# Expert stage of a two-layer decoder step: the next expert's rows are turned behind gate and up

## The reference

```
hid = silu(einsum('td,edf->tef', hf, w_gate)) * einsum('td,edf->tef', hf, w_up)
y   = einsum('tef,efd->td', hid * gate[..., None], w_down)
```

## Time and profile before

| what | value |
|---|---|
| median of 3 runs | 1547.96 us |
| the profiled execution | 1544.7 us |
| its span, first to last instruction | 1542.9 us |
| mean granted TensorE clock | 0.905 of full speed |
| TensorE busy with matmuls | 1246.5 us (81%) |
| VectorE, ScalarE, GpSimd busy | 567.9, 412.2, 168.8 us |
| GU in all 32 steps | 240.6 us busy, 44.5 us idle before it |
| moved by DMA | 270.85 MB, 176 GB/s over the span |

### The profile page before, as it was taken

The page is one execution under the profiler, slowest core; times in us unless marked ns, Lnnn a source line. Parts: engine busy times, 40 slices in busy tenths (PEclk is TensorE's granted clock), DMA queues, the critical chain, the costliest instruction groups (busy, mean ns, idle before and its releaser), DMA issues. The chain is left out here.

```text
span 1542.9 us, 22257 instructions
## 1 busy us (share of the span) xinstructions
PE 1246.5 (81%) x8931; PEld 1090.5 (71%) x8931; DVE 567.9 (37%) x1008; ACT 412.2 (27%) x861; POOL 168.8 (11%) x129
## 2 busy tenths in 40 slices
PE   1799999987999855888871999948997963888890
PEld 1799999986999755777751999924336953777770
DVE  2321223339522240111124537688665342111115
ACT  4423244442312320000013522237444240000002
POOL 0300000005000001000002017750000002000002
PEclk9899999998999957999995899958998956999995
DMA  8572322221232105888884138770551205888855
GB/s 242 218 265 82 108 84 83 82 95 50 68 106 83 55 28 212 325 323 326 326 295 156 56 126 285 246 255 28 197 185 64 75 0 221 298 321 318 320 214 203
DMA packets 113405, 270.85 MB, mean 176 GB/s; under 512 B 11094, under 2 KB 69742, under 8 KB 105134
## 3 DMA queue, kind: packets, MB, share of 16 engines
q1 hardware_dynamic: 92768, 230.77, 42.1%
q0 software_dynamic: 9424, 33.13, 5.7%
q10 hardware_dynamic: 11142, 5.96, 1.4%
HBM read 225.43 MB, written 44.40 MB: 175 GB/s over the span
## 5 line engine op out<-in xcount | busy, mean ns | idle before, releaser
L998 PE MATMUL ps<-hT_parts,wh 128*128 128x260 f32 x1152 | 326.8, 284 | 0.0
L1144 PE MATMUL ps<-U,ring 128*128 128x128 f32 x2048 | 240.6, 279 | 44.5 <-DVE U L1604 44.5
L1144 PEld LDWEIGHTS ps<-U,ring 128*128 128x128 f32 x2048 | 234.8, 194 | 52.1 <-issue 33.5
L1366 DVE TENSOR_TENSOR ring_parts<-ring,wh 128x1024 fp32r<-128x1024 f32 x104 | 136.6, 1315 | 263.0 <-ACT wh L710 263.0
L996 PE MATMUL ps<-x_parts,wh 128*128 128x260 f32 x768 | 219.6, 286 | 8.7 <-ACTq L749 7.9
L998 PEld LDWEIGHTS ps<-hT_parts,wh 128*128 128x128 f32 x1152 | 218.5, 190 | 0.0
L997 PE MATMUL ps<-x_parts,ring_parts 128*128 128x260 f32 x768 | 217.3, 283 | 0.0
L996 PE MATMUL ps<-V_parts,wh 128*128 128x260 f32 x512 | 147.8, 289 | 8.2 <-DVE U_parts L1482 5.2
L996 PEld LDWEIGHTS ps<-x_parts,wh 128*128 128x128 f32 x768 | 145.3, 189 | 9.1 <-ACTq L749 8.0
L997 PE MATMUL ps<-V_parts,ring_parts 128*128 128x260 f32 x512 | 146.5, 286 | 0.0
L997 PEld LDWEIGHTS ps<-x_parts,ring_parts 128*128 128x128 f32 x768 | 145.2, 189 | 0.0
(11 more groups left out here) (250 smaller groups left out, 1757.1 us busy)
## 6 DMA issues: line engine op xcount, KB each, us to landing
ring<-in_w_e_gate SPq DMA_DIRECT2D x32, 1024.0 KB, 5.0
ring<-in_w_e_up SPq DMA_DIRECT2D x32, 1024.0 KB, 7.7
ring<-in_w_e_down SPq DMA_DIRECT2D x32, 1024.0 KB, 8.6
ring<-in_w_uv SPq DMA_DIRECT2D x24, 1024.0 KB, 5.6
U<-slots_dram SPq DMA_DIRECT2D x32, 512.0 KB, 5.7
slots_dram<-U SPq DMA_DIRECT2D x32, 512.0 KB, 8.9
ring<-in_cache_k SPq DMA_DIRECT2D x32, 512.0 KB, 4.4
ring<-in_cache_v SPq DMA_DIRECT2D x32, 512.0 KB, 5.2
```

Source lines behind the costliest of these rows:

```text
L998: ins = pe.matmul(to, wh[:, chunk % 2, c, :], rhs_l(c, half), start=False, stop=last and c == DC - 1)
L1144: ins = pe.matmul(ps[:, 2 + q, f * SLOTS:(f + 1) * SLOTS], w[:, c, (f % 2) * P:(f % 2 + 1) * P], xsT[:, q, c, :], start=c == 0, stop=c == ...
L1366: e.tensor_tensor(low_parts(b, half), w, plain(wh[:, chunk % 2]), ALU.subtract).then_inc(split_lo, 1)
```

## The change

In three lists two neighbours change places, in the loop and in the experts written out ahead of it. On TensorE T(e+1) goes ahead of D(e-1), on VectorE evac(e+1) goes ahead of `y_half`(e-1), and on SyncE rows(e) goes ahead of the load of gate(e). No instruction is added or taken away, and the waits in front of each are the same; ScalarE's and GpSimd's lists do not change.

```diff
@@ SyncE, experts @@
                     else:
+                        load_rows(0, 2)
                         load(b, wg[2], (DC, DE))
-                        load_rows(0, 2)
                         load(b + 1, wu[2], (DC, DE))
                         load(b + 2, wd[1], (2, D))
                 with sp.Fori(0, 6) as i:
                     for k in range(2):
                         b = base + 8 + 3 * k
+                        load_rows(i, 3 + k)
                         load(b, one(wg, i * 2 + (3 + k)), (DC, DE), i, 2)
-                        load_rows(i, 3 + k)
                         load(b + 1, one(wu, i * 2 + (3 + k)), (DC, DE), i, 2)
                         load(b + 2, one(wd, i * 2 + (2 + k)), (2, D), i, 2)
                         store_rows(i, k)
+                load_rows(0, 15)
                 load(base + 44, wg[15], (DC, DE))
-                load_rows(0, 15)
@@ TensorE, moe_t @@
                 gate_up(0, 1, base + 2)
+                turn_rows(0, 2)
                 down(0, 0, base + 4)
-                turn_rows(0, 2)
                 gate_up(0, 2, base + 5)
+                turn_rows(0, 3)
                 down(0, 1, base + 7)
-                turn_rows(0, 3)
                 with pe.Fori(0, 6) as i:
                     for k in range(2):
                         b = base + 8 + 3 * k
                         gate_up(i, 3 + k, b)
+                        turn_rows(i, 4 + k)
                         down(i, 2 + k, b + 2)
-                        turn_rows(i, 4 + k)
@@ VectorE, moe_v @@
                     hidden(0, k)
+                    evac_rows(0, k + 1)
                     y_half(0, k - 1)
-                    evac_rows(0, k + 1)
                 with e.Fori(0, 6) as i:
                     for k in range(2):
                         hidden(i, 3 + k)
+                        evac_rows(i, 4 + k)
                         y_half(i, 2 + k)
-                        evac_rows(i, 4 + k)
```

## The result

The changed kernel takes 1500.76 us, the median of 4 runs (1497.73 to 1502.94), against 1548.18 us of the kernel before: a ratio of 0.969 (95% interval 0.967 to 0.971), 47.4 us less. In two later sets of five runs it was at 0.9705 (0.9683 to 0.9726) and 0.9708 (0.9682 to 0.9733), 45.4 and 45.9 us less. The forecast was 41.7 us less, 1506.3 us, with a range from 1501 us on: the direction and the mechanism hold, the forecast gain is too small, and the median lies 0.2 us outside of the range.

A forecast was written before the change was run, and what follows sets the result against it. It took the expert chain GU, D, T, evac, GU as the bound, with DMA not far behind. 28 x 1.52 less 1.0 us gave 41.7 us off the 1547.96 us median: 1506.3 us, range 1501 to 1515.

The forecast's parts named there:

- The bound and the starts that gain: In the expert stages the chain GU, D, T, evac, GU bounds; GU(2) to GU(15) lose their wait, 28 starts.
- The period: One expert's cycle on TensorE falls from 13.09 to 11.57 us, 1.52 us each, 42.7 us over 28.
- The bound below it: Lower bound of the expert period: 11.47 us without GU's slower first row behind a stall, a gain of 1.62 us.
- Layer 0's end: Next stage's weight blocks load 2.55 us later against GU(15), idle DMA fills 1.5: a loss of 1.0 us (0 to 2.55).
- The range: Whole kernel: 1501 to 1515 us, from 34 to 45 us of gain less 0 to 2.55 and 2 us of clock.
- The moved steps on VectorE and SyncE: In the expert loop D hides evac with 1.9 us to spare; the earlier rows load holds up nothing behind it.
- The slack: In the expert loop, rows(e) land 5.7 us after issue, 11.9 us before T(e) needs them.
- DMA as the bound: In the expert stages DMA sustains only 319 GB/s: about 1539 us, chance 0.06; the forecast took no cost, at 368 GB/s.
- the 2 us worked out from it: At 358 GB/s an expert's DMA batch takes 11.72 us; the gain is up to 2 us smaller, through layer 0's end.
- The rivals: For the expert stages: DMA bounds, about 1539 us (0.06); no gain, 1547 to 1549 (0.03); slower, 1577 (0.04).
- The slower one: In the expert stages DMA's slow 287 GB/s spreads over the batch, 14.6 us each: 1577 us in all, chance 0.04.

## Why the prediction was right in kind and too small

- **The bound and the starts that gain: right.** 28 of 32 waits for evac are gone, four are left at 5.9 us in all.
- **The period: the step that failed.** The forecast went by GU's 7.25, T's 0.88 and D's 3.44 us and took 28 x 1.52 (1.524 unrounded) = 42.7 us, "because the parts 7.25 and 3.44 hold joins of their own already". The bound below it, 11.47 us without the 0.1 us that GU takes longer behind a stall, is what happened: 11.46 us, 1.63 us a period, 45.8 us in all, 3.1 more than taken. GU's part was measured behind a stall, and the stall was what the change removed; three times the evac's work brings stall and 7.25 us back together. The two new joins cost nothing: 0.88 from T's start to D's, 3.43 from D's to GU's.
- **Layer 0's end:** 1.0 us forecast, 0.6 measured.
- **The range:** both together put the forecast at 45.2 us less, 1502.8 us, inside the range; the two later sets (45.4 and 45.9) meet it. The first set's 47.4 us stand 2 us above that. I take these for scatter, which is argued and not shown: the changed kernel's medians are 1500.8, 1501.2 and 1501.5 us, those of the kernel before 1548.2, 1546.6, 1546.3 and 1547.4, with single runs of it from 1538.5 to 1549.2. One place where runs of the changed kernel differ is GU(0) of layer 1, where the clock rises: 8.80 us long in the first profile, 10.28 and 10.33 in the two later ones (8.75 in the kernel before). That the first median fell just outside of the range was chance; the term was too small in every set.
- **The moved steps on VectorE and SyncE:** 2.0 us of cover against 1.9 forecast; the moved load is worth nothing that these runs can tell, as a large slack said (it still has time when issued late). The slack itself was put too high, 11.9 us against 7.1, mostly because rows take 9.5 us to land now and not 5.7.
- **DMA as the bound:** no cost taken, rightly, but from a wrong number. The 368 GB/s of the earlier trace rows are not what DMA can do: it moved 413 without a wait, and 418 as a bound. The Trainium skill's 358 GB/s for each core (DMA: Bandwidth & Descriptors, Specifications) is passed by all three, so the 2 us worked out from it did not come.
- **The rivals:** none happened. The slower one's slow stretches did not spread: the rate over the stage is 362 GB/s. Its 287 GB/s of the earlier trace rows was not the slowest microsecond there, as that heading says; the next one, from 651 us, had 258.

## What to carry to other kernels

Where an engine waits for the copy of its own last result, put independent work that is long enough between the two, and move the copying engine's list along with it: here TensorE's list moved without VectorE's lost 19.5 us. A part that is timed behind a stall holds the stall's restart; when the stall goes, that goes too, so time such parts where they run without one. A DMA share of 0.98 did not say how much was left; an added load of known size did.

## What the runs showed of the hardware that was not expected

With VectorE's old order the granted clock fell in the middle of layer 1's experts. GU there took 9.01 us, where 7.41 is usual, behind a wait of 2.12 us:

```profile
1326.15 3.60 PE L1162 MATMUL ps<-ring,U 128*128 128x512 f32 x8
1331.87 9.01 PE L1144 MATMUL ps<-U,ring 128*128 128x128 f32 x64 [2.12 <-DVE U L1604]
```

```profile
1331.00:1336.00 5.00, 4.13 (x22) 4.16 (x23) 0.61 (x1) 0.00 (x0) 0.00 (x0) 0.66 0.90 318
```

The mean of 0.66 over 5 us is part full clock, 2.4 GHz, and part 1.2 GHz. It happened at two of the 28 starts (the other behind a wait of 1.99 us), for 3.2 us in all; the rest of the 28, with waits of about 2 us too, kept the full clock. With the 17.9 us that the longer periods make in this profile that is about the 20.8 us that the profiled run, 1567.35 us, stands above the kernel before. Whether the other runs had such starts is not shown; two of the four are 17.6 and 18.2 us above, as if without. The waits of 1.3 to 1.5 us in the kernel before never cost the clock in its profile.

Longer waits did it again. With twice evac's work, GU(1) of layer 0 stands behind 2.65 us:

```profile
609.73 9.01 PE L1144 MATMUL ps<-U,ring 128*128 128x128 f32 x64 [2.65 <-DVE U L1608]
```

With three times the work it takes 9.01 us behind 3.78 us in both layers, while with twice the work a wait of 2.68 us in layer 1 left it at 7.38. So a wait of some 2 us or more inside a busy stage can cost more than its own length.
